# A two-layer hybrid encoder step: value products of two cycles joined, maxima further ahead, output weights split early through memory

## The chip, the cores and the metric

The kernel runs on one core of a Trainium2 chip. The metric is the device time of one execution in microseconds (us), as the median of several runs. A core has a matrix engine (TensorE, PE, with a weight load of its own, PEld), a vector engine (VectorE, DVE), an activation engine (ScalarE, ACT), a general engine (GpSimd, POOL) and an engine that here only issues DMA (SyncE, SP). Each works through its own queue in order and waits on semaphores.

## What is computed

One inference step of one layer for 2048 prompt positions and 8 samples of 16 positions, model width 1024. The layer normalises its input, makes one combined projection, runs three mixers beside each other, and projects their gated outputs back:

```
h = rms_norm(x, norm_g)
fq, fk, fv, fg, ff, su, sg, mq, mg = split_columns(h @ w_in)
fox_out = fox_attend(fq, fk, fv, logf).reshape(B, T, FOX_WIDTH) * jax.nn.silu(fg)
ssm_out = ssm_y * jax.nn.silu(sg)
mem_out = memory_attention(mq, mem_k, mem_v).reshape(B, T, MEM_WIDTH) * jax.nn.silu(mg)
mix = jnp.concatenate([fox_out, ssm_out, mem_out], axis=-1) @ w_out
return x + mix
...
s = einsum(q, k) * HEAD_DIM ** -0.5 + cq - ck          # fox: 8 heads of 64, causal
p = softmax(where(mask, s, -inf));  out = einsum(p, v)
```

The memory attention has four heads of 64 into 256 tokens without a mask. Products of f32 quality are made of three products of rounded halves (high by high, high by low, low by high), so the operands, `w_out` among them, are split into a high half (fp32r) and a low half.

## The kernel before, in words

Three stages follow one another. The projection (up to about 790 us of the profile) goes through passes of 17 position tiles, "visits"; `projection_order` writes down an order of steps that every engine follows, and `beside` hangs other steps on a visit's three parts. The attention of the prompt (790 to 1237 us) and the output product (to the end) are both in `attention_and_output`, whose order comes from `attention_order`.

**The attention's order.** A head has six units (`UNITS`): for the forgetting attention four query groups of four tiles with 4, 8, 12 and 16 key tiles, for the memory attention two groups with two blocks of keys each. That is 44 blocks a head, 352 in all; a cycle is four of them, so a head has 11 cycles and the kernel 88, numbered from 0. The last unit of a head ("fox 12") has cycles 7 to 10 of it; in the last head these are cycles 84 to 87. In a cycle PE does four scores (`scores`: two products each, transposed, keys by queries, L2487 and L2492, and a mask product L2489 on the diagonal), then four maxima (`top`, L2470: the scores again in the other direction, only for their maximum per query), and the value products of the same four blocks (`values`, L2518: 16 products of 64 output columns, 256 queries wide). DVE reduces the maxima (L2828), the negated maxima are turned by PE (`row`, L2481) and copied by ACT (L2607) into a spare row of the query tensor, and the first score of a unit waits for that. ACT then takes the exponential (L2618). The probabilities are summed into denominators by adds (L2788, L2790) on POOL, and for key blocks 2, 3, 6 and 10 of the long units on DVE; `both` (L2841) joins the two sums on DVE, `den` turns them on PE (L2500) and reduces them on DVE (L2847).

**Banks.** `Ring` gives scores, maxima, rows and denominators six banks of PSUM in turn: an entry takes the bank used longest ago and waits until ACT or DVE has emptied it. The exponentials go into 16 slots, four cycles' worth.

**Numbers that set the order.** `LEAD` is how many maxima are issued in the first cycles (four in each later one), and with the 12 issued at three `HOOKS` in the last visits of the projection it sets how far maxima run ahead of scores. `TOGETHER` is over how many cycles the value products are gathered.

**The output weights.** `w_raw` is loaded once (8 chunks of 128x1024). In heads 1 to 4 POOL makes four sums and differences of them per head (`t_sums`, L2734 to L2739), which SP stores. In the last head ACT copies each chunk in two halves into the high part `w_hi` (`w_split`, L2636), which lies over the query and key tensors of the even heads, and POOL subtracts it for the low part (`w_low`, L2743); likewise for the sums (`t_split`, L2648, `t_low_early`, L2747). The first output products, ("product", 0, 0) and (0, 1) (L2586), wait for all of it. Their left side is the mix, loaded tile by tile, turned on PE (`mix`, L2541) and gated on POOL (`gated`, L2721); `first_sum` (L2895) is DVE's sum of the first of them.

**SP's queue.** For every head from 2 on SP issues 7 loads of queries and keys when the head before the last has its scores done (`load_queries_keys`), 8 loads of values and memory tensors (`load_values`), and 4 stores of outputs (`store`).

## Time and profile before

| What | us |
| --- | --- |
| median of 3 runs (1432.9 to 1437.66) | 1434.78 |
| the profiled execution | 1428.78 |
| its span | 1427.1 |
| busy in the span: PE / PEld | 1383.0 / 1101.7 |
| busy in the span: DVE / ACT / POOL | 926.3 / 635.2 / 559.8 |
| product groups of L927, the projection (three groups) | 331.3, 321.7, 234.6 |
| value products L2518 (1216 on the fox values) | 144.8 |
| mean DMA rate over the span | 193 GB/s |

The profile is of one execution. A timeline row gives start, duration, engine, line, operation, output and inputs and how many instructions were merged, and in brackets how long the engine sat idle before and on what. A matmul's duration runs into that of the next one, as they are pipelined; what one costs in a run is the distance between starts.

### The profile page before, as it was taken

How to read it: one execution, taken by the hardware profiler on the slowest of the kernel's cores; microseconds unless marked ns; L12 is line 12 of the kernel's file. 1: busy time of each engine (PE TensorE's matmuls, PEld its weight loads, DVE VectorE, ACT ScalarE, POOL GpSimd, SP SyncE). 2: the span in 40 equal slices, each digit the busy share in tenths (PEclk: the TensorE clock that was granted, in tenths of full speed). 3: DMA queues.
4: the chain of work that ended last, by engine and by line, in shares of the span. 5: the costliest groups of instructions: out<-in, count | busy, mean ns of one | idle time of the engine just before them, and what ended most of it. 6: DMA issues, size and time to landing. Idle time of an engine off the chain costs nothing.

```text
span 1427.1 us, 25010 instructions
## 1 busy us (share of the span) xinstructions
PE 1383.0 (97%) x8510; PEld 1101.7 (77%) x8510; DVE 926.3 (65%) x1772; ACT 635.2 (45%) x1364; POOL 559.8 (39%) x587
## 2 busy tenths in 40 slices
PE   8999989999999999999999999999999999799998
PEld 8999767788877767777777777777777777578886
DVE  4789755692466787665333766676676666697784
ACT  6766423432443364445332555555554556432221
POOL 1121432200033243212000566676775659544442
PEclk9999999999999999999999999999999999899999
DMA  7885699987369679678996945725726514346552
GB/s 230 304 285 189 221 250 243 321 260 211 91 162 326 206 224 301 220 251 261 333 294 187 247 126 113 156 56 116 156 57 130 125 33 126 98 152 217 181 186 86
DMA packets 207565, 275.82 MB, mean 193 GB/s; under 512 B 49424, under 2 KB 146096, under 8 KB 203952
## 3 DMA queue, kind: packets, MB, share of 16 engines
q1 hardware_dynamic: 206400, 274.22, 65.8%
q8 instruction: 70, 1.15, 0.3%
q14 instruction: 55, 0.45, 0.1%
q10 hardware_dynamic: 1040, 0.00, 0.0%
HBM read 186.93 MB, written 86.00 MB: 191 GB/s over the span
## 4 chain that ended last, share of the span: by engine, by line
PE 59%; DVE 5%; issue 2%; POOL 2%; ACT 2%; DMA 1%; SPq 1%; DVEq 0%; ACTq 0%; POOLq 0%
PE in_g L927 13%; PE attn_pv L2518 11%; PE attn_s L2487 6%; PE attn_s L2586 6%; PE attn_s L2492 5%; PE attn_s L2470 5%; PE attn_pv L2586 4%; PE attn_s L2500 2%; PE in_b L1102 1%; POOL in_hv L1810 1%; PE in_b L1054 1%; PE attn_s L2489 1%; PE attn_s L2473 1%; PE attn_s L2541 1%; PE in_b L1157 1%
## 5 line engine op out<-in xcount | busy, mean ns | idle before, releaser
L927 PE MATMUL in_g<-in_wh,in_xh 128*128 128x512 f32 (+2 forms) x904 | 331.3, 380 | 4.9 <-DVE in_wl L1521 1.9
L927 PE MATMUL in_g<-in_wl,in_xh 128*128 128x512 f32 (+2 forms) x904 | 321.7, 369 | 0.0
L2828 DVE TENSOR_REDUCE attn_tops<-attn_s 128x1 f32<-128x512 f32 (+3 forms) x288 | 159.7, 617 | 126.6 <-PE attn_s L2470 110.3
L927 PE MATMUL in_g<-in_wh,in_xl 128*128 128x512 f32 (+2 forms) x904 | 234.6, 378 | 1.4 <-DVE in_xl L1532 1.3
L2790 POOL TENSOR_TENSOR attn_probs<-attn_probs,attn_probs_turned 128x512 f32<-128x512 f32 (+3 forms) x190 | 202.1, 1064 | 86.1 <-ACT attn_probs_turned L2618 64.1
L2618 ACT ACTIVATE attn_probs_turned<-attn_s 128x512 f32<-128x512 f32 (+1 forms) x352 | 161.4, 545 | 144.9 <-PE attn_s L2492 144.6
L927 PEld LDWEIGHTS in_g<-in_wh,in_xh 128*128 128x128 f32 x904 | 165.5, 189 | 39.7 <-issue 6.2
L927 PEld LDWEIGHTS in_g<-in_wl,in_xh 128*128 128x128 f32 x904 | 165.5, 189 | 28.0
L927 PEld LDWEIGHTS in_g<-in_wh,in_xl 128*128 128x128 f32 x904 | 157.8, 189 | 34.4 <-issue 5.2
L1808 POOL TENSOR_SCALAR in_hs<-in_hs 128x8 f32<-128x8 f32 (+1 forms) x53 | 21.3, 402 | 398.6 <-DVE in_hs L1559 398.6
L2518 PE MATMUL attn_pv<-attn_probs_turned,attn_v 128*64 128x256 f32 (+1 forms) x1216 | 144.8, 368 | 0.1
L1219 ACT ACTIVATE in_xh<-in_xu 128x512 fp32r<-128x512 f32 x174 | 99.7, 623 | 57.7 <-DMA in_xu<-scratch_xt 57.7
L2518 PEld LDWEIGHTS attn_pv<-attn_probs_turned,attn_v 128*64 128x64 f32 x1216 | 85.8, 138 | 42.3 <-issue 11.2
L1532 DVE TENSOR_TENSOR in_xl<-in_xu,in_xh 128x512 fp32r<-128x512 f32 x106 | 68.6, 688 | 37.2 <-ACT in_xh L1219 33.7
L1810 POOL TENSOR_TENSOR in_hv<-in_hs,all_neghalf 128x8 f32<-128x8 f32 (+1 forms) x53 | 83.8, 1581 | 4.4
L2487 PE MATMUL attn_s<-attn_qa,attn_ka 128*128 128x512 f32 (+3 forms) x160 | 62.6, 391 | 6.0 <-DVE attn_den L2847 6.0
L2788 POOL TENSOR_TENSOR attn_probs<-attn_probs_turned 128x512 f32<-128x512 f32 x39 | 51.5, 1329 | 39.4 <-ACT attn_probs_turned L2618 39.4
L1260 ACT ACTIVATE in_x_turned<-in_tr 128x512 fp32r<-128x512 f32 (+1 forms) x53 | 27.5, 519 | 85.2 <-PE in_tr L949 76.0
L2487 PE MATMUL attn_s<-all_x,all_y 128*128 128x512 f32 (+3 forms) x160 | 62.1, 388 | 1.6 <-DVE attn_tops L2828 1.6
L2492 PE MATMUL attn_s<-attn_qb,attn_kb 100*128 100x512 f32 (+3 forms) x160 | 61.7, 386 | 0.0
L2492 PE MATMUL attn_s<-all_x,all_y 100*128 100x512 f32 (+3 forms) x160 | 61.0, 381 | 0.0
L1579 DVE TENSOR_TENSOR in_work<-in_g,in_hr 128x512 f32<-128x512 f32 (+1 forms) x53 | 31.4, 593 | 38.4 <-POOL in_hr L1813 37.5
(379 smaller groups left out, 2716.3 us busy)
## 6 DMA issues: line engine op xcount, KB each, us to landing
in_xu<-scratch_xt SPq DMA_DIRECT2D x87, 512.0 KB, 5.5
in_xl<-scratch_xt SPq DMA_DIRECT2D x34, 512.0 KB, 4.6
in_raw<-in_w_in SPq DMA_DIRECT2D x40, 256.0 KB, 5.3
scratch_xt<-in_xu SPq DMA_DIRECT2D x19, 512.0 KB, 4.6
scratch_xt<-in_xl SPq DMA_DIRECT2D x17, 512.0 KB, 4.5
scratch_k<-in_x_turned SPq DMA_DIRECT2D x17, 512.0 KB, 7.0
scratch_q<-in_x_turned SPq DMA_DIRECT2D x17, 512.0 KB, 5.3
in_x_turned<-in_x_prompt SPq DMA_DIRECT2D x16, 512.0 KB, 4.7
```

The lines of the kernel that those rows point to most:

```text
L927: last = X.matmul(g_ps[b][:, 0:m], x, ws[:, c, w0:w0 + m], start=(c == 0 and h == 0 and ws is wh), stop=(c == KC - 1 and h == 1))
L1219: F(xh[:, item_visit[j] % 2, 4 * h:4 * h + 4, :], xu[:, j % 2, 4 * h:4 * h + 4, :], ACT.Copy)\
L1532: V.tensor_tensor(xl[:, v % 3, 4 * h:4 * h + 4, :], xu[:, j % 2, 4 * h:4 * h + 4, :], fl(xh[:, v % 2, 4 * h:4 * h + 4, :]), ALU.subtract). ...
L1810: G.tensor_tensor(hv[:, 0:m], hs[:, 0:m], K.neghalf[:, 0:m], ALU.pow).then_inc(s_hchain, 1)
L2470: last = X.matmul(bank[:, at:at + n, :], qb[h][0:LANE, q], kb[h][0:LANE, keys], start=True, stop=not masked)
L2487: X.matmul(bank[:, part:, :], y2[h][:, keys], x2[h][:, q], start=True, stop=False)
L2492: X.matmul(bank[:, part:, :], y1[h][0:FULL, keys], x1[h][0:FULL, q], start=False, stop=True)\
L2518: last = X.matmul(v_ps[u.n % 2][lane * HD:(lane + 1) * HD, tiles[0] // 2:EACH // 2, :], vals[:, k, :], pt[:, s % SLOTS, tiles[0]::2, :], s ...
L2586: last = X.matmul(y_ps[at], ms[left][:, c, :], ws, start=(begins and c == 0 and k == 0), stop=(ends and c == HALF - 1 and k == 2))
L2618: F(pt[:, s % SLOTS, at:, :], ring_ps[ring.at["scores", s]][:, at:, :], ACT.Exp).then_inc(s_exp, 1)
L2790: E.tensor_tensor(acc[:, part:, :], acc[:, part:, :], mine, ALU.add).then_inc(added[engine], 1)
L2828: V.tensor_reduce(top_parts[:, joined[u.n] % 2, i, k // 4:k // 4 + 1], bank[:, 0:n, :].rearrange("p n k -> p (n k)"), AX.X, ALU.max).then_ ...
```

## The change

It does five things.

1. `TOGETHER` becomes 2: the value products of an even cycle are made with those of the odd one behind it, except in cycles 86 and 87. Denominators are turned at these points only.
2. `LEAD` becomes six for all of the first six cycles, 36 maxima instead of 32, and the three hooks with the first 12 maxima (and row 0) move from behind parts 1 and 2 of the last visit and its end to behind part 2 of the visit before and parts 0 and 1 of the last.
3. In the last unit DVE no longer makes all adds: POOL and DVE share them as in other long units, and `both` for it stands ahead of the first output product, `first_sum` between the first two, `den` behind them.
4. `w_split` and `w_low` work on 16 halves of 128x512, one after each cycle of `W_AT` (17, 20, ... 62, that is in heads 1 to 5). The high half goes into one staging tile `w_stage`, from where POOL subtracts and SP stores it (`store_w`) to memory; SP loads all of `w_hi` back when head 6's scores are done. ACT waits before each copy for the subtraction and the store of the half before (and for the sums made of the chunk).
5. The first two parts of the `t_split` and `t_low_early` move to cycles 78 and 80.

```diff
@@ before_attention
-    for n in range(HOOKS - 1):
-        beside[NV - 1, n + 1] = [("attention", n)]
-    order = projection_order(items, visits, behind, beside) + [("attention", HOOKS - 1)]
+    for n, at in enumerate(((NV - 2, 2), (NV - 1, 0), (NV - 1, 1))):
+        beside[at] = [("attention", n)]
+    order = projection_order(items, visits, behind, beside)
...
-CYCLE, TOGETHER = 4, 1
+CYCLE, TOGETHER = 4, 2
...
-LEAD = (6, 6, 5, 5, 5, 5)
+LEAD = (6, 6, 6, 6, 6, 6)
+W_CHUNKS = (0, 4, 1, 5, 2, 6, 3, 7)
+W_AT = (17, 20, 23, 26, 29, 32, 35, 38, 41, 44, 47, 50, 53, 56, 59, 62)
@@ Sums
-            late = u.head == FOX_HEADS - 1 and u.blocks > 12
-            mine = [k for k, _ in u.scores if u.kind == "fox" and (late or u.blocks > 8 and k in (2, 3, 6, 10))]
+            mine = [k for k, _ in u.scores if u.blocks > 8 and k in (2, 3, 6, 10)]
@@ attention_order
-        if 1 <= n <= KC:
-            order += [("w_split", n - 1, 0), ("w_split", n - 1, 1), ("w_low", n - 1)]
-        if n in (KC, KC + 1):
-            order += [("t_split", n - KC), ("t_low_early", n - KC)]
+        if c in W_AT:
+            order += [(what, W_AT.index(c)) for what in ("w_split", "w_low", "w_out")]
+        if n in (1, 3):
+            order += [("t_split", n // 2), ("t_low_early", n // 2)]
...
-    order += [("product", 0, 0), ("product", 0, 1)] + [("den", n) for n in ended[cycles - 1]]
-    order += [("first_sum", 0), ("t_split", 2), ("t_split", 3), ("mix", 1)]
+    order += [("both", n) for n in ended[cycles - 1]] + [("product", 0, 0), ("first_sum", 0), ("product", 0, 1)]
+    order += [("den", n) for n in ended[cycles - 1]] + [("t_split", 2), ("t_split", 3), ("mix", 1)]
@@ attention_and_output
-        stage = sums_raw[:, 0:2, :]
+        stage, w_stage = sums_raw[:, 0:2, :], sums_raw[:, 2, :]
...
+        def store_w(sp, n):
+            cols = slice(n % 2 * 512, (n % 2 + 1) * 512)
+            sp.wait_ge(s_wh, n + 1)
+            sp.dma_start(D.w_hi[W_CHUNKS[n // 2]][:, cols], w_stage).then_inc(s_w_out, 16)
@@ sync_program, for each head behind store(sp, head - 2)
+                for x in order:
+                    if x[0] == "w_out" and head - 1 == W_AT[x[1]] // (head_end(0) // CYCLE):
+                        store_w(sp, x[1])
@@ sync_program, behind store(sp, FOX_HEADS - 2)
+            sp.wait_ge(s_score, head_end(FOX_HEADS - 2))
+            sp.wait_ge(s_w_out, 16 * 2 * KC)
+            for c in range(KC):
+                sp.dma_start(fl(w_hi[c]), D.w_hi[c]).then_inc(s_w[c % HALF], 16)
@@ tensor_steps, ("product", 0, 0)
-                        pe.wait_ge(s_wl, KC)
+                        pe.wait_ge(s_wl, 2 * KC)
+                        for c in range(HALF):
+                            pe.wait_ge(s_w[c], 16 * 4)
@@ scalar_steps, w_split
-                    act.wait_ge(s_t, 4 * (s % HALF + 1))
-                    act.wait_ge(s_score, head_end(FOX_HEADS - 2))
-                    cols = slice(rest[0] * 512, (rest[0] + 1) * 512)
-                    F(w_hi[s][:, cols], w_raw[:, s, cols], ACT.Copy).then_inc(s_wh, 1)
+                    c, cols = W_CHUNKS[s // 2], slice(s % 2 * 512, (s % 2 + 1) * 512)
+                    act.wait_ge(s_t, 4 * (c % HALF + 1))
+                    if s:
+                        act.wait_ge(s_wl, s)
+                        act.wait_ge(s_w_out, 16 * s)
+                    F(w_stage.bitcast(F32R), w_raw[:, c, cols], ACT.Copy).then_inc(s_wh, 1)
@@ gpsimd_program, w_low
-                    pool.wait_ge(s_wh, 2 * (c + 1))
-                    G.tensor_tensor(w_lo[:, c, :], w_raw[:, c, :], fl(w_hi[c]), ALU.subtract).then_inc(s_wl, 1)
+                    pool.wait_ge(s_wh, s + 1)
+                    G.tensor_tensor(w_lo[:, c, cols], w_raw[:, c, cols], w_stage, ALU.subtract).then_inc(s_wl, 1)
```

How the queues change at three places. First PE between the cycles 6 and 7 of head 0. L2470 and L2473 (L2485 and L2488 after) are maxima, L2481 (L2496) a row, L2518 value products, L2487 and L2492 (L2502 and L2507) scores. Before:

```order
2806 L2470 MATMUL attn_s<-attn_kb,attn_qb 128x512
2807 L2473 MATMUL attn_s<-attn_causr,attn_identr 128x128
2808 L2481 MATMUL attn_s<-attn_identr,attn_negmax 128x128
2809 L2518 MATMUL attn_pv<-attn_probs_turned,attn_v 64x256 x2
2810 L2518 MATMUL attn_pv<-attn_probs_turned,attn_v 64x128
2811 L2518 MATMUL attn_pv<-attn_probs_turned,attn_v 64x256
2812 L2518 MATMUL attn_pv<-attn_probs_turned,attn_v 64x128 x3
2813 L2487 MATMUL attn_s<-all_x,all_y 128x512
2814 L2492 MATMUL attn_s<-all_x,all_y 128x512
```

After:

```order
2811 L2488 MATMUL attn_s<-attn_causr,attn_identr 128x128
2812 L2496 MATMUL attn_s<-attn_identr,attn_negmax 128x128 x2
2813 L2502 MATMUL attn_s<-all_x,all_y 128x512
2814 L2507 MATMUL attn_s<-all_x,all_y 128x512
2815 L2502 MATMUL attn_s<-all_x,all_y 128x512
2816 L2507 MATMUL attn_s<-all_x,all_y 128x512
2817 L2502 MATMUL attn_s<-all_x,all_y 128x512
2818 L2507 MATMUL attn_s<-all_x,all_y 128x512
2819 L2502 MATMUL attn_s<-all_x,all_y 128x512
2820 L2507 MATMUL attn_s<-all_x,all_y 128x512
```

The value products of cycle 6 have gone from between the two cycles to behind the maxima of cycle 7. Second, ACT in cycles 46 to 48: exponentials (L2618, L2635 after), rows (L2607, L2624), copies of values (L2629, L2646). Before:

```order
670 L2618 ACTIVATE attn_probs_turned<-attn_s 128x128
671 L2607 ACTIVATE attn_qb<-attn_s,all_ident 4x128 x4
672 L2629 ACTIVATE attn_out<-attn_pv 128x256
673 L2618 ACTIVATE attn_probs_turned<-attn_s 128x512 x4
674 L2629 ACTIVATE attn_out<-attn_pv 128x256 x2
675 L2618 ACTIVATE attn_probs_turned<-attn_s 128x512 x9
```

After:

```order
658 L2635 ACTIVATE attn_probs_turned<-attn_s 128x128
659 L2635 ACTIVATE attn_probs_turned<-attn_s 128x512 x4
660 L2646 ACTIVATE attn_out<-attn_pv 128x256 x3
661 L2655 ACTIVATE attn_sums_raw<-attn_w_raw 128x512
662 L2635 ACTIVATE attn_probs_turned<-attn_s 128x512 x8
663 L2624 ACTIVATE all_x<-attn_s,all_ident 4x128 x4
```

The copies of three units' values are now together behind the exponentials of cycle 47, and behind them the split L2655 into the staging tile stands ahead of the eight exponentials of cycles 48 and 49. Third, DVE in the last unit: adds (L2788 and L2790; L2807 and L2809 after), joining of the two sums (L2841; L2860), denominators (L2847, L2851; L2866, L2870), low halves of the mix (L2885; L2904), `first_sum` (L2914 after). Before:

```order
1074 L2790 TENSOR_TENSOR attn_acc_v<-attn_acc_v,attn_probs_turned 128x256
1075 L2841 TENSOR_TENSOR attn_acc_v<-attn_acc_v,attn_probs 128x512
1076 L2788 TENSOR_TENSOR attn_acc_v<-attn_probs_turned 128x512
1077 L2790 TENSOR_TENSOR attn_acc_v<-attn_acc_v,attn_probs_turned 128x512 x6
1078 L2847 TENSOR_REDUCE attn_den<-attn_s 128x4
1079 L2851 RECIPROCAL attn_rfox<-attn_den 128x4
1080 L2790 TENSOR_TENSOR attn_acc_v<-attn_acc_v,attn_probs_turned 128x512 x4
1081 L2885 TENSOR_TENSOR attn_qb<-attn_s,attn_qa 128x512
1082 L2885 TENSOR_TENSOR attn_qb<-attn_raw_ka,attn_qa 128x512
1083 L2790 TENSOR_TENSOR attn_acc_v<-attn_acc_v,attn_probs_turned 128x512
1084 L2790 TENSOR_TENSOR attn_acc_v<-attn_acc_v,attn_probs_turned 128x384
1085 L2790 TENSOR_TENSOR attn_acc_v<-attn_acc_v,attn_probs_turned 128x256
```

After:

```order
1072 L2807 TENSOR_TENSOR attn_acc_v<-attn_probs_turned 128x512
1073 L2809 TENSOR_TENSOR attn_acc_v<-attn_acc_v,attn_probs_turned 128x512
1074 L2866 TENSOR_REDUCE attn_den<-attn_s 128x4
1075 L2870 RECIPROCAL attn_rfox<-attn_den 128x4
1076 L2809 TENSOR_TENSOR attn_acc_v<-attn_acc_v,attn_probs_turned 128x512
1077 L2904 TENSOR_TENSOR attn_qb<-attn_s,attn_qa 128x512
1078 L2904 TENSOR_TENSOR attn_qb<-attn_raw_ka,attn_qa 128x512
1079 L2860 TENSOR_TENSOR attn_acc_v<-attn_acc_v,attn_probs 128x512
1080 L2914 TENSOR_TENSOR attn_x_even<-attn_s,attn_x_even 128x512 x2
1081 L2866 TENSOR_REDUCE attn_den<-attn_s 128x4
1082 L2870 RECIPROCAL attn_rfox<-attn_den 128x4
1083 L2880 TENSOR_TENSOR attn_a_raw<-attn_s,attn_probs 128x512
```

Of 16 adds on DVE four are left; the joining sum of this unit is new, and the first sum stands ahead of the last denominators.

## Rows read from the trace of the kernel before

**Rows 1.** Windows: length, busy PE, PEld, DVE, ACT, POOL, PEclk, DMA, GB/s.

```profile
1000.00:1100.00 100.00, 100.00 (x672) 76.43 (x670) 67.14 (x124) 51.40 (x132) 69.63 (x63) 1.00 0.55 118
...
1180.00:1220.00 40.00, 38.01 (x245) 27.16 (x244) 25.05 (x42) 27.93 (x62) 37.58 (x28) 1.00 0.41 114
```

**Rows 2.** Timeline, PE, one cycle: start, us, engine, line.

```profile
896.44 0.22 PE L2481 MATMUL attn_s<-attn_identr,attn_negmax 128*128 128x128 f32 x1
896.60 1.95 PE L2518 MATMUL attn_pv<-attn_probs_turned,attn_v 128*64 128x256 f32 x16
898.47 0.50 PE L2487 MATMUL attn_s<-attn_qa,attn_ka 128*128 128x512 f32 x1
898.81 0.22 PE L2489 MATMUL attn_s<-attn_identr,attn_causr 128*128 128x128 f32 x1
```

**Rows 3.** Waits of the weight loads, 795 to 1211 us: us, times, longest.

```profile
PEld attn_s L2487 <- issue: 23.2, 73, 0.4
```

**Rows 4.** Timeline, PE, end of attention, idle in brackets.

```profile
1219.94 0.84 PE L2500 MATMUL attn_s<-all_ident,attn_acc_v 128*128 128x128 f32 x4 [1.93 <-DVE attn_acc_v L2841]
1220.71 3.37 PE L2518 MATMUL attn_pv<-attn_probs_turned,attn_v 128*64 128x256 f32 x16
...
1234.80 0.69 PE L2487 MATMUL attn_s<-attn_qa,attn_ka 128*128 128x384 f32 x1 [6.00 <-DVE attn_den L2847]
...
1236.99 1.50 PE L2541 MATMUL attn_s<-all_ident,attn_out 128*128 128x128 f32 x6
...
1240.97 0.50 PE L2586 MATMUL attn_s<-all_x,attn_qa 128*128 128x512 f32 x1
...
1249.53 0.47 PE L2586 MATMUL attn_s<-all_x,attn_qa 128*128 128x512 f32 x1 [1.62 <-DVE attn_x_even L2895]
```

**Rows 5.** Timeline, PE and ACT, start of attention.

```profile
791.37 0.50 PE L2487 MATMUL attn_s<-all_x,all_y 128*128 128x512 f32 x1 [1.64 <-DVE attn_tops L2828]
...
787.28 0.69 ACT L1242 ACTIVATE in_work<-in_g,in_half 128x512 f32<-128x512 f32 x1 [6.00 <-PE in_g L927]
789.85 1.12 ACT L2607 ACTIVATE all_x<-attn_s,all_ident 4x128 fp32r<-4x128 f32 x4 [1.88 <-PE attn_s L2481]
```

**Rows 6.** Timeline, DVE, last unit's adds.

```profile
1222.66 11.48 DVE L2790 TENSOR_TENSOR attn_acc_v<-attn_acc_v,attn_probs_turned 128x512 f32<-128x512 f32 x6
...
1234.88 3.06 DVE L2790 TENSOR_TENSOR attn_acc_v<-attn_acc_v,attn_probs_turned 128x512 f32<-128x512 f32 x4
```

**Rows 7.** Timeline, POOL, gating of the third mix tile.

```profile
1249.18 1.04 POOL L2721 TENSOR_TENSOR attn_out<-attn_out,attn_rfox 128x512 f32<-128x512 f32 x1 [16.38 <-DMA attn_out<-scratch_mem_gate]
```

**Rows 8.** Windows, the granted clock: PEclk, the third number from the end.

```profile
1220.00:1224.00 4.00, 4.00 (x20) 2.10 (x20) 3.90 (x2) 0.68 (x1) 4.00 (x2) 0.57 0.01 4
...
1234.80:1238.40 3.60, 3.60 (x15) 3.29 (x15) 2.83 (x5) 1.15 (x3) 0.00 (x0) 0.50 0.02 6
```

**Rows 9.** Timeline, POOL and PE, cycles 16 to 18.

```profile
874.20 4.11 POOL L2790 TENSOR_TENSOR attn_probs<-attn_probs,attn_probs_turned 128x512 f32<-128x512 f32 x3 [3.55 <-ACT attn_probs_turned L2618]
880.14 3.21 POOL L2790 TENSOR_TENSOR attn_probs<-attn_probs,attn_probs_turned 128x512 f32<-128x512 f32 x3 [1.82 <-ACT attn_probs_turned L2618]
...
887.28 1.82 POOL L2739 TENSOR_TENSOR attn_sums_raw<-attn_w_raw,attn_t_raw 128x512 f32<-128x512 f32 x1
...
883.13 0.50 PE L2487 MATMUL attn_s<-attn_qa,attn_ka 128*128 128x512 f32 x1
```

**Rows 10.** Timeline, SP and PE, heads 3 and 4.

```profile
1010.21 0.48 SPq L2229 DMA_DIRECT2D attn_qb<-scratch_q  x1
...
1034.29 0.69 SPq L2262 DMA_DIRECT2D scratch_mem_t<-attn_out  x1
...
1032.10 0.50 PE L2487 MATMUL attn_s<-all_x,all_y 128*128 128x512 f32 x1
```

**Rows 11.** DMA issues, 790 to 1200 us: KB each, us to landing.

```profile
scratch_t<-attn_sums_raw SPq DMA_DIRECT2D x8, 256.0 KB, 2.2
...
scratch_fox_t<-attn_out SPq DMA_DIRECT2D x14, 256.0 KB, 3.7
```

5 lines of the change are left out of this document (3 added, 2 removed).

## The prediction

> **What bounds the kernel now.** I read the page first, then busy time by stretches, the order of time on TensorE, the waits, and the order of time on the other engines. The profiled execution took 1428.8 us for a span of 1427.1 us, 6.0 us under the median of the runs shown, 1434.8 us; the steps below are worked out on the profiled execution, and the difference is taken off the median. In the middle of the attention TensorE (PE) is busy without a break: 100.00 us of 100 [rows 1]. There only less work on PE, or a new wait on it, changes the time; an edit on ACT, DVE, POOL or SP counts only if PE is made to wait or stops waiting. Towards the end of the attention this is over: 38.01 of 40 us, with POOL busy 37.58 [rows 1], and behind it come the long idle stretches of [rows 4]. They are the second place where time can be won.
>
> **1. Cycles joined, 88 value groups become 45.** The value products (a 128x64 tile) stand between products with full 128-column tiles. In the cycle of [rows 2] PE goes from a 128-column product at 896.44 to the first value product at 896.60, 0.16 us, where 128 columns take 0.06 (the 16 value products of 256 columns each start within 1.87 us, 0.117 apiece): 0.10 lost on the way in. Behind the values the first score product holds PE for 0.34 us (898.47 to 898.81), where its 512 columns take 0.23 at that rate: 0.11 lost on the way out. The waits show it too: between 795 and 1211 us the weight load of that product starts late 73 times, 23.2 us in all [rows 3]. 43 groups go, one of them in the last unit, which I work out apart: 42 x 0.20 = 8.4 us. The lower bound is 42 x 0.10, if a new loss from maxima to scores takes half of it back (the trace of before has that seam only once, under a wait); the upper is 8.8. I take 8.4, since each seam is seen in the trace at its size. The adds, exponentials and maxima are unchanged in number, so nothing else is removed here.
>
> **2. First maxima sooner and four more of them ahead.** Before the first scores PE sits idle 1.64 us, until DVE empties a bank [rows 5]. With the maxima ahead of the last product, DVE is through in time; but then the first scores need row 0, which ACT copies only behind its step on the last product. That step starts at 787.28, takes 0.6 us until the next can start, and the four copies take 1.12 us [rows 5]: 2.0 us behind the end of the product at 787.1. The maxima and the row that PE did in between, 2.4 us, are now ahead of the product. So the product ends 2.6 us later and the scores follow 2.0 us behind it with one bank product in the shadow: the wait changes its name, and the time is the same within 0.3 us. The four maxima further ahead cost no work; they give slack to rows in the middle and put six maxima per cycle on DVE in cycles 2 to 5, six banks in back-to-back scores and maxima; I count 0.7 us of waits for it.
>
> **3. The last unit.** Before, the last unit's 16 adds are all DVE's. They wait for DVE to take over POOL's sum of the unit before, which is late because POOL makes eight low halves of the weights among its adds (busy 37.58 of 40 us, [rows 1]); then six adds of full width take 11.48 us, 1.91 each, where four more take 3.06, 0.77 each, once POOL is done [rows 6]. PE waits 1.93, 6.00 and 1.62 us [rows 4]. Behind the first two the granted clock is 0.57 and 0.50 of full speed, the lower of the two levels (1.2 GHz against 2.4) [rows 8]: the values at 1220.71 take 3.37 us for 1.95 [rows 2, 4], 1.42 lost, and the stretch from 1234.80 to 1240.97, 6.17 us [rows 4] at about half clock, loses 3.05. That is 14.0 us. In the changed kernel POOL has no weight halves in the last head, takes 11 adds of the last unit and DVE four. Three adds with a neighbour on DVE take 3.2 us when one is narrow and 4.1 when all are wide [rows 9], against 3.9 us of PE for a cycle without maxima (eight products of 0.23 and the values' 1.95): POOL ends some 3 us behind the last scores, DVE's joining sum at about 4.5, and PE comes to the last transposes only behind two products, 8.1 us behind them. So the cover is over 3 us wide. The first sum moves ahead of the denominators, so the 1.62 goes as well. What is late next: the transposes of the third mix tile need POOL's product, which starts at 1249.18 when a DMA lands [rows 7], 12.2 us behind the end of the last scores at 1237.0 [rows 4]; the loads ahead of it, two of 1 MB among them, still start only with the last scores. PE would get there at 12.1 us and POOL's two products end at 13.8: 1.7 us come back. Net 14.0 - 1.7 = **12.3 us**, between 10 and 14.
>
> The Trainium skill, "SBUF — State Buffer", section "Who interferes with whom", says that a DVE instruction with two SBUF inputs contends with a GpSimd instruction that reads SBUF. Its summary of the shared pair is an exclusive lock for a whole instruction. [Rows 6] agree in kind. By the lock each DVE add beside POOL's would hold POOL up for its whole 0.77 us, where the 4.1 us for three POOL adds hold a part of that already. POOL would fall back by at most 0.8 us in each of three cycles, 2.4 us of a cover of over 3 us, and rival B below would weigh a little more; the sum would stay.
>
> **4. Weight halves in heads 1 to 5, through one staging tile.** 16 ACT copies and POOL subtractions of 128x512 replace 16 copies and 8 subtractions of 128x1024. Their own time is hidden: ACT is busy 51.40 and POOL 69.63 of 100 us [rows 1]. Their waits are another matter, for each stands in ACT's queue ahead of the next cycle's exponentials, and PE can only do four scores and two maxima (2.6 us) before it needs a bank that those exponentials empty. An exponential ends 1.2 us behind the release, so ACT may be 1.4 us late at the start of a cycle at no cost.
> - Cycle 17: the copy waits for four sums on POOL that end at 889.1 [rows 9]. Joined, POOL goes from cycle 16's adds to 17's without its 1.82 us idle: 887.3. Cycle 18 starts at 883.13 [rows 9] less 0.2, or 882.9. So ACT is held until 4.4 us into cycle 18, the copy ends at 5.0, the first exponential at 5.5, where PE wants the bank at 2.6: PE waits 2.9 us.
> - Cycle 47: the copy waits until the half before it is in memory. Its store stands in SP's queue behind the loads of a head, which SP takes 24.8 us to issue (1010.21 to 1034.98) [rows 10], its queue being full. They start when head 3's last scores are done. Cycle 48 starts 21.9 us later (1032.10) [rows 10]; joined, those scores lie 2.0 us further ahead and 0.4 is saved: 23.5. ACT is there at 24.3, SP at 24.8, and the store lands 2.2 us later at the least [rows 11], or 3.7 if it takes as long as a store into a full queue: at 27.0 or 28.5. The exponential ends 1.3 us behind that, PE wants the bank at 26.1: it waits 2.2 to 3.7, I take 2.9.
> - Cycles 26, 38 and 59 meet the same queue, but ACT comes later or SP sooner there: 0.5 us together. Where two rows are copied (twice the 1.12 us of [rows 5]) inside a joined pair, at cycles 20, 42 and 64, 1.0 us.
> - With the 0.7 us of part 2: 2.9 + 2.9 + 0.5 + 1.0 + 0.7 = 8.0 us. Bounds: 0, if ACT's lateness is absorbed, and 16, if each estimate is half of what comes.
> - A wait of 2.9 us may lower the clock behind it. After 1.93 us idle it fell, after 1.64 it did not [rows 5, 8]; a fall cost 1.42 us and 0.24 more on the transposes. I count one of two: 1.7 us, bounds 0 and 3.4.
> - The 4 MB read back start with head 7, when no other head is loaded; before, 4 MB landed while attention ran on. They are needed over 40 us later: nothing. The mix loads behind them come some 10 us later, still ahead of POOL's step in cycle 81.
>
> **Sum.** 8.4 + 12.3 - 8.0 - 1.7 = 11.0 us off: a span of about 1416 us, and **1423.8 us** as a median.
>
> **Rivals.**
> - *A: the waits of part 4 don't reach PE.* For it: PE shows no wait at all between 795 and 1211 us ([rows 3] has late weight loads only); against it: with values held back PE has less to do ahead of the bank. 1423.8 - 9.7 = 1414.1 us.
> - *B: POOL remains late in the last head.* Its work there is some 30 us of the 32 us ahead of the last unit, and PE's transposes for unit 46 need POOL's adds of cycle 83. If gating the first mix tile waits for its loads behind the 4 MB, everything behind it slides; beyond 3 us the last sum is late as well, and the 6.00 us wait with its clock loss comes back: 9.3 us less, 1433.1 us, no change.
> - *C: slower. Each joined pair waits for a bank.* Scores, maxima, scores, maxima follow one another through six banks, while DVE needs 2.4 us for four maxima and up to 1.9 us for an add beside POOL. I find 0.2 to 0.9 us of slack at the third maximum of the second cycle. If that is 0.5 us short in each of 43 pairs, 21.5 us are added: 1445.3 us. It decides from 0.26 us per pair on; above 0.36 the kernel is slower by over 0.3%. Against it: DVE is busy 67.14 of 100 us [rows 1], and the banks that the maxima take were given to the same engine three microseconds before.
> - *D: halfway,* the waits of part 4 twice as long, the store's landing above all: 1431.8 us.
>
> **Chances.** Forecast 0.50, A 0.18, B 0.12, C 0.07, D 0.13. The range goes from a little below A, 1412.5, to just short of D, 1431.0. A measurement of this kernel can tell about 0.3%, 4.3 us, from no change: faster is below 1430.5. The forecast with its own spread (1417 to 1430) and A are there, with a part of D: 0.76. Within 0.3%: B, most of D, the rim of the forecast: 0.17. Slower: C: 0.07.
>
> **What would show it.** Right: a mean of about 4.89 us per cycle for 4.99; "issue" waits of the score weight load about 37 times for 73; PE waits named after ACT's exponential just behind the cycles 17 and 47; POOL's eight 128x1024 subtractions gone from the last head, and no idle PE from the last unit's scores to its first product over 1 us; a wait for row 0 of about 1.6 us at the start. Wrong: many short waits on PE inside the pairs (C); POOL busy without a break before the last unit and its sum late (B); or ACT waiting for SP and PE none the less busy (A).

## The result, and the profile after

| | before | after |
| --- | --- | --- |
| median, us | 1434.78 (1432.9 to 1437.66, 7 runs) | 1448.04 (1442.29 to 1453.31, 7 runs) |
| ratio | | 1.0089, 95% interval 1.0075 to 1.0103 |
| profiled execution, its span | 1428.78, 1427.1 | 1453.31, 1451.3 |
| mean granted clock of that execution | 0.996 | 0.984 |

The kernel became slower by 13.3 us; the forecast was that it would be 11.0 us faster. The two profiles differ by 24 us, more than the medians, because that of before (1428.78 us) lies below all seven executions in the table and that of after is the slowest of its seven. The sizes below are those of the profiled pair.

The page first, the busy lines and the 40 slices of the granted clock:

```profile
PE 1396.3 (96%) x8510; PEld 1120.9 (77%) x8510; DVE 913.5 (63%) x1761; ACT 637.7 (44%) x1364; POOL 572.9 (39%) x606
...
PEclk9999999999999999999999999999989899999999
```

PE does the same 8510 matmuls, but is busy 13 us longer (1383.0 before), though its value products stand in 43 groups fewer: busy time grows where the clock is low. The projection is the same (busy 759.41 us of the first 785, 758.02 before), and from the first output product to the end PE takes 187.7 us for 186.1. All the rest is in the attention, from the first scores behind row 0 to the first product: 791.13 to 1263.59 us here, 791.37 to 1240.97 before [rows 4, 5], 472.5 us for 449.6.

The waits of PE there (us in total, times, longest; the 1.63 us for row 0, the longest at L2507, lie just ahead of the stretch and are not counted in its sum):

```profile
PE attn_s L2485 <- ACT attn_probs_turned L2635: 15.1, 10, 3.6
PE attn_s L2507 <- ACT all_x L2624: 3.0, 3, 1.6
PE attn_s L2515 <- DVE attn_acc_v L2860: 0.9, 2, 0.7
PE attn_s L2496 <- ACT attn_probs_turned L2635: 0.5, 3, 0.2
PE attn_s L2502 <- ACT attn_probs_turned L2635: 0.3, 2, 0.2
```

Before, PE had no wait between 795 and 1211 us. Now maxima wait for a bank that ACT's exponentials have to empty. Six of the ten waits stand behind a split of the output weights and make up 13.9 us: 2.62, 0.83, 2.14, 2.95, 3.56 and 1.82, behind cycles 17, 20, 26, 38, 47 and 59. The largest, on PE, ACT and SP (start, us, engine, line; idle before it in brackets):

```profile
1058.96 1.28 PE L2485 MATMUL attn_s<-all_y,all_x 66*128 66x512 f32 x2 [3.56 <-ACT attn_probs_turned L2635]
...
1057.79 0.63 ACT L2655 ACTIVATE attn_sums_raw<-attn_w_raw 128x512 fp32r<-128x512 f32 x1 [4.52 <-DMA scratch_w_hi<-attn_sums_raw]
1058.33 2.04 ACT L2635 ACTIVATE attn_probs_turned<-attn_s 128x512 f32<-128x512 f32 x4
...
1029.20 0.48 SPq L2232 DMA_DIRECT2D attn_qb<-scratch_q  x1
...
1034.54 13.04 SPq L2247 DMA_DIRECT2D attn_mqa<-scratch_mq  x2
...
1053.81 4.99 SPq L2323 DMA_DIRECT2D scratch_w_hi<-attn_sums_raw  x2
```

Read it from the last row up. SP issues a head's loads from 1029.20 on and is stopped for 13.04 us among them; the store of the staged half is issued at 1053.81, 24.6 us after the first load (24.8 was the forecast). ACT has wanted to overwrite the staging tile since 1053.27 and stands until the store has landed, 3.9 us behind its issue. The four exponentials of the next cycle are queued behind the copy, so PE gets its bank at 1058.96. All of ACT's waits at this line, by what they were for:

```profile
ACT attn_sums_raw L2655 <- DMA scratch_w_hi<-attn_sums_raw: 15.3, 4, 4.5
...
ACT attn_sums_raw L2655 <- POOL attn_sums_raw L2758: 6.1, 2, 3.6
```

Then the clock. Windows of 4 us of PE (length, busy, PEclk, DMA share, GB/s), around the waits of cycles 17 and 47:

```profile
888.00:892.00 4.00, 2.31 (x11) 1.00 0.00 0
892.00:896.00 4.00, 3.07 (x8) 0.50 0.17 66
896.00:900.00 4.00, 4.00 (x22) 0.65 0.00 0
...
1056.00:1060.00 4.00, 1.04 (x2) 0.90 0.32 120
1060.00:1064.00 4.00, 4.00 (x13) 0.50 0.00 1
1064.00:1068.00 4.00, 4.00 (x19) 0.50 0.02 4
1068.00:1072.00 4.00, 4.00 (x31) 0.82 0.00 0
```

At both the clock goes from 2.4 to 1.2 GHz, for 6.8 and for 10.2 us (each window's length times its missing share, over one half). It does so at the waits of cycles 17, 26, 38, 47 and 59, which are all five of more than 1.8 us, and once more at the start, behind the 1.63 us. At cycles 17, 26 and 38 it goes down already in the last 0.6 to 1.6 us of the wait, at the other two 0.3 and 1.4 us behind it. Together PE is at the lower level for 47.8 us of the attention, for 10.2 before. Half of what PE is busy of it is lost: 21.9 us (3.9 of the 47.8 are idle), for 4.7 before.

So the attention of the profiled pair comes out as: waits 18.2 us for 7.9, + 10.3; clock + 17.3; the joining - 6.3 (experiment e20). That is 21.3 of the 22.9 us by which the stretches differ; a rest of about the remaining 1.6 us shows again in e20, and its cause is open. The last unit, the other half of the forecast, did what was expected of it: no wait of PE over 0.25 us from the last unit's scores to the first product.

### The profile page after: what moved, and what is told of

It reads as the page before. It is cut to its first block, busy times and chain, and to the rows that moved or that the text cites. A ratio compares the mean times of both kernels' runs of the same rounds, so it can differ in the third digit from the quotient of the medians.

```text
span 1451.3 us, 25044 instructions
## 1 busy us (share of the span) xinstructions
PE 1396.3 (96%) x8510; PEld 1120.9 (77%) x8510; DVE 913.5 (63%) x1761; ACT 637.7 (44%) x1364; POOL 572.9 (39%) x606
## 4 chain that ended last, share of the span: by engine, by line
PE 49%; SPq 6%; DVE 5%; ACT 4%; issue 3%; DMA 3%; POOL 2%; ACTq 0%; DVEq 0%; POOLq 0%
PE in_g L927 13%; PE attn_pv L2533 8%; PE attn_s L2603 5%; PE attn_pv L2603 4%; SPq L2247 3%; PE attn_s L2502 3%; PE attn_s L2507 3%; PE attn_s L2485 3%; ACT attn_probs_turned L2635 2%; PE attn_s L2515 2%; PE in_b L1102 1%; DMA scratch_w_hi<-attn_sums_raw 1%; POOL in_hv L1810 1%; SPq L2265 1%; PE in_b L1054 1%
## 5 line engine op out<-in xcount | busy, mean ns | idle before, releaser
L2809 POOL TENSOR_TENSOR attn_probs<-attn_probs,attn_probs_turned 128x512 f32<-128x512 f32 (+3 forms) x200 | 215.7, 1079 | 91.9 <-ACT attn_probs_turned L2635 68.5
L2847 DVE TENSOR_REDUCE attn_tops<-attn_s 128x1 f32<-128x512 f32 (+3 forms) x288 | 160.3, 617 | 143.9 <-PE attn_s L2485 123.6
L2635 ACT ACTIVATE attn_probs_turned<-attn_s 128x512 f32<-128x512 f32 (+1 forms) x352 | 162.3, 545 | 103.7 <-PE attn_s L2507 102.5
L2533 PE MATMUL attn_pv<-attn_probs_turned,attn_v 128*64 128x256 f32 (+1 forms) x1216 | 138.2, 369 | 0.0
L2533 PEld LDWEIGHTS attn_pv<-attn_probs_turned,attn_v 128*64 128x64 f32 x1216 | 91.0, 140 | 40.2 <-issue 9.4
L2507 PE MATMUL attn_s<-all_x,all_y 100*128 100x512 f32 (+3 forms) x160 | 63.3, 396 | 3.0 <-ACT all_x L2624 3.0
L2807 POOL TENSOR_TENSOR attn_probs<-attn_probs_turned 128x512 f32<-128x512 f32 x40 | 52.4, 1318 | 29.3 <-ACT attn_probs_turned L2635 29.3
L2502 PE MATMUL attn_s<-all_x,all_y 128*128 128x512 f32 (+3 forms) x160 | 63.2, 395 | 0.2 <-ACT attn_probs_turned L2635 0.2
L2502 PE MATMUL attn_s<-attn_qa,attn_ka 128*128 128x512 f32 (+3 forms) x160 | 62.9, 393 | 0.2 <-ACT attn_probs_turned L2635 0.2
L2507 PE MATMUL attn_s<-attn_qb,attn_kb 100*128 100x512 f32 (+3 forms) x160 | 63.0, 394 | 0.0
L2485 PE MATMUL attn_s<-all_y,all_x 66*128 66x512 f32 (+3 forms) x160 | 49.3, 404 | 12.4 <-ACT attn_probs_turned L2635 12.1
```

Of the source, the lines that this page charges most:

```text
L2485: last = X.matmul(bank[:, at:at + n, :], qb[h][0:LANE, q], kb[h][0:LANE, keys], start=True, stop=not masked)
L2502: X.matmul(bank[:, part:, :], y2[h][:, keys], x2[h][:, q], start=True, stop=False)
L2507: X.matmul(bank[:, part:, :], y1[h][0:FULL, keys], x1[h][0:FULL, q], start=False, stop=True)\
L2533: last = X.matmul(v_ps[u.n % 2][lane * HD:(lane + 1) * HD, tiles[0] // 2:EACH // 2, :], vals[:, k, :], pt[:, s % SLOTS, tiles[0]::2, :], s ...
L2635: F(pt[:, s % SLOTS, at:, :], ring_ps[ring.at["scores", s]][:, at:, :], ACT.Exp).then_inc(s_exp, 1)
L2809: E.tensor_tensor(acc[:, part:, :], acc[:, part:, :], mine, ALU.add).then_inc(added[engine], 1)
```

## Experiments

Ratios are to the kernel before, run beside each kernel on the same chip; its median was 1432.0 (e1, e3, e4, e5), 1434.4 (e9, e10, e11, e13) and 1433.3 us (e14 to e20). Kernels that ran on different chips are compared by these ratios. A trace is one execution of a kernel, and its waits and clock need not be those of the next one.

### Is it the splits, or the joining?

e1_join is the kernel before with `TOGETHER` 2:

```diff
-CYCLE, TOGETHER = 4, 1
+CYCLE, TOGETHER = 4, 2
```

> The kernel before, with the cycles joined in pairs and nothing else of the change. Theory Q (the change lost its time to the splits of the output weights in heads 1 to 5, which stop ACT behind a store or a sum, and to the clock that falls behind each such wait; the joining itself works): 1427 to 1430 us, 5 to 8 us under the kernel before, no new waits of PE in the middle of the attention and a granted clock of 1.00 there. Rival J (the joining itself costs: PE waits for banks inside the pairs, or the joined values pull the clock down): 1440 us or more, with short PE waits in every second cycle.

Measured: 1438.8 us, ratio 1.0038 (1.0024 to 1.0052). Neither theory was right. No wait for a bank in the pairs is longer than 0.2 us, but there are five for a row, and the clock falls at the very start:

```profile
791.23 0.80 PE L2487 MATMUL attn_s<-all_x,all_y 128*128 128x512 f32 x1 [1.64 <-DVE attn_tops L2828]
798.67 0.79 PE L2492 MATMUL attn_s<-all_x,all_y 100*128 100x512 f32 x1 [0.67 <-ACT all_x L2607]
...
944.92 0.50 PE L2492 MATMUL attn_s<-all_x,all_y 100*128 100x512 f32 x1 [0.93 <-ACT all_x L2607]
...
792.00:796.00 4.00, 4.00 (x19) 0.50 1.04 254
...
800.00:804.00 4.00, 4.00 (x13) 0.50 1.03 225
```

Up to 791.2 us this kernel issues the same instructions as the kernel before and waits the same 1.64 us [rows 5], yet here the clock is at its lower level for 17 us and there not at all. The execution of before that was profiled had a mean clock of 0.996; its 20 runs beside this kernel had 0.990 to 0.993. So the profile on which the forecast was built lacked low clock that all 20 have. e18_adders below, which is the kernel before up to the last head, has a fall of 10.2 us at this place in its trace, with a mean clock of 0.991. A fall here is therefore the likely reason for the 6 us between the profile of before and the median; no trace of an ordinary execution of that kernel was kept that would show it.

e9_join_lead adds the lead of the change, six maxima in each of the first six cycles.

> The kernel before with cycles in pairs and six maxima in each of the first six cycles (e1_join with the lead of the change). e1_join showed PE waiting 0.93 us for a row in every second head and 0.67 at the start, 5.3 us in all. Theory L (these waits are a lead that is four banks too short): they go, 1432 to 1435 us, where e1_join had 1438.8. Rival (the row waits come from the pairs as such): 1437 to 1440 us, as e1_join. For the joining by itself both say that a head of 11 cycles takes 54.1 to 54.3 us where it is undisturbed, for 54.88 before: 0.12 us per pair, not 0.20.

Measured: 1434.75 us, ratio 1.0000 (0.9984 to 1.0016). In e1_join the waits for rows were 0.67 and four times 0.93, 4.4 us in all (not the 5.3 of the text above). Two of 0.68 are left, and 0.70 and 0.27 of other kinds: four more maxima of lead are needed as soon as cycles are joined. Joined and with its lead, the kernel is as fast as before, not faster.

e3_spaced is the changed kernel with the splits at other cycles:

```diff
-W_AT = (17, 20, 23, 26, 29, 32, 35, 38, 41, 44, 47, 50, 53, 56, 59, 62)
+W_AT = (18, 20, 23, 29, 31, 35, 40, 42, 46, 51, 53, 57, 62, 64, 68, 73)
```

> The changed kernel with the sixteen splits at cycles 18, 20, 23, 29, 31, 35, 40, 42, 46, 51, 53, 57, 62, 64, 68 and 73: none is ahead of the store of the one before it when that store stands behind the loads of a head in SP's queue, and the first isn't in the cycle of POOL's sums. Work and bytes are the same. Theory Q: the PE waits behind the splits (13.9 us in six places) and five falls of the clock (some 20 us) go: 1413 to 1422 us. Rival J: 1440 us or more. Rival W (the sixteen splits cost by their work on ACT and POOL, wherever they stand): between, 1430 to 1440 us.

Measured: 1420.43 us, ratio 0.9919 (0.9898 to 0.9941), as theory Q has it. The same work and the same bytes, at other places, are worth some 24 us (the difference of the two ratios). Rival J and rival W, the work of the splits wherever they stand, are both out. ACT waits for no store any more, and the first product starts at 1232.43 us, for 1263.59. What is left behind splits are three waits of 0.83 us, where a split and two rows fall into the first cycle of a pair, two of them with the clock low behind them.

e5_c17 moves only the first split, from cycle 17 to 18.

> The changed kernel with only the first split moved from cycle 17 to cycle 18; ACT waited 3.56 us there for POOL's sums and PE 2.62 us, and the clock was at its lower level for about 6.8 us behind it. Theory Q: that wait and that fall go, 5 to 6.5 us: 1441.5 to 1443 us, and the granted clock is 1.00 between 885 and 905 us. Rival J: no change, 1446 to 1450 us, since the fall comes from something else.

Measured: 1438.97 us, ratio 1.0059 (1.0039 to 1.0078), 4.3 us less than the change by the ratios (5 to 6.5 expected, and the two intervals overlap a little); the wait of 2.62 us and its fall are gone from the trace. It doesn't price that wait alone: behind cycle 38 PE waits 0.57 us here and not 2.95, behind cycle 59 1.05 and not 1.82, while the fall at the start lasts 13.7 us for 6.8, and the ten executions range from 1434.5 to 1446.0 us. So the waits at the other splits move when one split moves.

e16_one_wait puts one wait back: e11's places (below), the fourth split at 26 instead of 29. It has the hooks of the change and not those of e11; PE's wait for row 0 is 1.63 us with either.

> e11's places of the splits, with the fourth split at cycle 26 instead of 29, where its wait for a store behind the head loads is back, and the hooks of the change. One such wait by itself. Theory Q: ACT waits some 3.6 us for the store, PE some 2.1, and the clock is at its lower level for 7 us behind it: 5 to 6 us more than e11_odd_sooner, 1423 to 1426 us. Rival J: the wait costs its 2.1 us alone, and the falls in the changed kernel come from joined cycles: 1420 to 1421.5 us.

Measured: 1428.94 us, ratio 0.9974 (0.9957 to 0.9991), for 0.9878 of e11 and 0.9895 of e20, which is the same kernel as e11: 11 to 14 us, and not 5 to 6. The rows show why:

```profile
943.42 0.63 ACT L2655 ACTIVATE attn_sums_raw<-attn_w_raw 128x512 fp32r<-128x512 f32 x1 [9.51 <-DMA scratch_w_hi<-attn_sums_raw]
...
944.59 0.69 PE L2485 MATMUL attn_s<-attn_kb,attn_qb 66*128 66x384 f32 x1 [8.04 <-ACT attn_probs_turned L2635]
...
940.00:944.00 4.00, 0.00 (x0) 0.58 0.54 157
944.00:948.00 4.00, 3.41 (x14) 0.50 0.17 66
```

The split at cycle 21 sits so late in its head that SP, which stores that half ahead of the next head's loads, begins these loads at 914.78 (910.65 in the changed kernel), and all behind them comes later; the store that the split at 26 waits for is issued at 939.29, not 935.57. The wait of 2.14 us became 8.04. With that and the fall behind it (10.2 us at the lower level, 3.9 of them idle, so 3.2 lost), 11 us are told by this trace, what the comparison with e20 gives. Rival J, the wait without a fall, is out: the fall is there, and e4_single (below) has such falls in single cycles too.

### The queue, or the places?

e17_sp_order leaves the splits of the change where they are, and issues a head's first store ahead of the next head's loads and the second among them (`soon` holds the splits in the first six cycles of a head; its definition is left out here, as is the loop over the stores that follow):

```diff
+                for n in soon[:1]:
+                    store_w(sp, n)
                 load_queries_keys(sp, head)
+                for n in soon[1:]:
+                    store_w(sp, n)
                 load_values(sp, head)
```

> The changed kernel with all its splits where they are, but SP's queue in another order: the store of a head's first split ahead of the next head's query and key loads, the second's between those and the value loads. Theory Q: the waits at cycles 26, 38, 47 and 59 (10.5 us of PE) and four falls of the clock go, the wait at cycle 17 for POOL's sums stays: 1422 to 1430 us, and ACT waits for no store for more than 1 us. Rival P (the splits wait because of where they stand among the adds and exponentials, not because of SP's queue): 1440 us or more. If the loads now come too late for the next head, PE waits for DMA at the start of heads 3 to 6: 1435 us or more.

Measured: 1448.86 us, ratio 1.0111 (1.0091 to 1.0131). No faster, yet the question is answered by the rows:

```profile
ACT attn_sums_raw L2661 <- POOL attn_sums_raw L2764: 6.0, 2, 3.6
...
PE attn_s L2491 <- DMA all_y<-scratch_k: 8.0, 2, 6.7
PE attn_s L2491 <- ACT attn_probs_turned L2641: 4.6, 6, 2.6
PE attn_s L2491 <- DMA attn_ka<-scratch_k: 4.0, 1, 4.0
```

ACT waits for no store, so SP's queue was the cause (theory Q, not P). But now the keys come too late, and PE stands 12 us for them at the head's maxima: the third case of what was expected. What this edit saved in ACT's waits it lost in PE's for the keys.

### What the last unit owes to what

e13_spaced_late is e3_spaced with all sixteen adds of the last unit on DVE, as before.

> e3_spaced with the last unit's sixteen adds on DVE alone, as in the kernel before; POOL has no low halves of the weights to make in the last head here either. If DVE's single-handed adds are the cause of the wait for the last sum (1.91 us each beside POOL), PE waits 3 to 6 us behind the last transposes and the clock falls: 1425 to 1431 us. If POOL's halves in the last head were the cause and not who adds, PE waits under 1.5 us: 1420 to 1422 us.

Measured: 1418.92 us, ratio 0.9898 (0.9871 to 0.9925), no slower than e3. DVE's adds (start, us, count):

```profile
1224.33 4.67 DVE L2810 TENSOR_TENSOR attn_acc_v<-attn_acc_v,attn_probs_turned 128x512 f32<-128x512 f32 x6
```

That is 0.78 each where [rows 6] show 1.91 beside POOL. POOL has nothing to do in that stretch, and then it doesn't matter who adds.

e18_adders is the other half: the kernel before with POOL's eleven adds and the new order at the end, the halves still in the last head.

> The kernel before with two edits of the change alone: POOL takes its eleven adds of the last unit, and the end of the order is the changed kernel's. The halves of the weights stay in the last head. Theory H (what frees the last unit is POOL without the halves): POOL is late with its adds as before, 1432 to 1437 us, no change, or slower, and PE still waits 4 us or more in all between the last unit's scores and the first product. Rival A (the division of the adds and the order do it): 1420 to 1426 us.

Measured: 1432.23 us, ratio 0.9989 (0.9975 to 1.0004), no change:

```profile
1213.97 1.65 PE L2469 MATMUL attn_s<-attn_kb,attn_qb 66*128 66x512 f32 x3 [4.29 <-DVE attn_den L2846]
1253.32 1.09 PE L2499 MATMUL attn_s<-all_ident,attn_acc_v 128*128 128x128 f32 x4 [7.29 <-DVE attn_acc_v L2840]
```

The second wait is for the last joined sum, which stands until POOL has done its adds at 1251.6 us, with halves of the weights between them. The first is for a sum of denominators on DVE, which stands behind an add of 128x512 that took 6.81 us (from 1206.50) while POOL went from one instruction to the next without a break. Together they are 11.6 us, where [rows 4] had 9.6 in three waits. Theory H holds: the gain of the last unit comes from the halves that left the last head, and the other two edits give nothing without them.

e10_spaced_single is e3_spaced with single cycles.

> e3_spaced (splits at cycles where no store is awaited) with single cycles. If the joining gives 0.12 us for each of 43 pairs in a kernel without other disturbance, 5 us more than e3_spaced: 1424 to 1428 us. If the joining is worth the 8.4 us of the prediction, 1428 to 1431 us. If it costs as much in waits and clock as it gives, 1418 to 1422 us.

Measured: 1421.2 us, ratio 0.9911 (0.9884 to 0.9938), like e3. It also sizes the last unit without anything joined: from the last head's memory scores to the first product it takes 34.8 us (1200.33 to 1235.13), before 48.75 (1192.22 to 1240.97): 13.95. The forecast's 14.0 hold 1.62 us that lie behind the first product; up to it 12.4 were forecast. And of the 13.95 some 1.0 us is the lead's: this stretch has 8 maxima here and 12 before.

e4_single is the changed kernel with single cycles, all splits where they were.

> The changed kernel with single cycles as before, everything else of the change kept. Theory Q: the waits behind stores stay, the gain of the joining is lost: 1450 to 1456 us, or down to 1440 us if single cycles leave ACT more slack, so that some waits don't reach PE (values lie between the scores then). Rival J: 1425 us or less, with a clock of 0.99 or more.

Measured: 1439.8 us, ratio 1.0053 (1.0038 to 1.0068). It is 5 us faster than the change, not slower: the second case of what was expected. The profiled execution is one of the quick ones of ten (clock 0.995, where they range from 0.987 to 0.995), so it may show fewer falls than most. In it PE's waits behind splits are 4.12, 0.52, 4.94 and 0.81 us (cycles 17, 26, 47 and 59), and none at 38: the number of larger ones goes from five to two, and so does that of the falls. Cycles 26 and 38 are the first of a pair: behind their copies PE has the next scores and no value products to do. So the joining had a part in the loss after all: 5 us by the ratios, and by the trace not through waits of its own but by letting the splits' waits reach PE.

### The start, and the best version

e11_odd_sooner has the splits in second cycles of pairs only (19, 21, 23, 29, 31, 35, 41, 43, 45, 51, 53, 57, 63, 65, 67, 73) and the first maxima one product sooner still; e20_odd_joined is the same kernel again, e19_odd_single the same with single cycles.

> The changed kernel with splits in second cycles of pairs only (19, 21, 23, 29, 31, 35, 41, 43, 45, 51, 53, 57, 63, 65, 67, 73), and the three groups of first maxima one product sooner still. Theory Q: the three waits of 0.83 us that e3_spaced still has behind a split and two rows in one cycle go, with the two short falls of the clock behind them (5.6 us at the lower level), and the 1.63 us for row 0 go to under 0.3: 1412 to 1417 us, for 1420.4 of e3_spaced. Rival: the maxima that are sooner still hold up the last projection product by as much (their banks are emptied by DVE between its own steps): 1418 to 1421 us.

> e11_odd_sooner with single cycles and nothing else. By the head lengths in the traces (54.11 us in e11 where nothing disturbs it, 54.89 in single cycles) the joining is worth 0.14 us per pair, 6.1 us in 43 pairs, less 2.0 us of waits for rows that only joined cycles show. So this kernel should be 3 to 5 us above e20_odd_joined, 1421 to 1424 us. Rival: the clock falls more often or longer at the start in joined cycles and takes the rest: within 2 us of e20.

> The same kernel as e11_odd_sooner, once more, beside e19_odd_single on the same chip: 1416 to 1420 us, ratio 0.986 to 0.990.

Measured: e11 1418.82 us, ratio 0.9878 (0.9845 to 0.9911); e20 1417.4 us, 0.9895 (0.9872 to 0.9918); e19 1418.77 us, 0.9900 (0.9878 to 0.9922). The three waits of 0.83 are gone. Joined against single, on one chip: 1.4 us, within what can be told from nothing, as the rival had it. The traces split this up. Two heads take 108.18 us joined (867.07 to 975.26) and 109.80 single, 0.147 us per pair, 6.3 in 43. But from the first scores to the first product it is 434.4 us for 436.4. Of the 4.3 that are missing, 2.1 are four waits for rows, a sum and a bank that single cycles don't have. The other 2.2 lie mostly in the first fourteen cycles: these take 2.2 us more instead of 1.0 less, and only 1.2 of that are waits. I can't place this rest. The clock is no part of it there: 1.00 in both.

The joining gives less than forecast because it makes a new seam. In e20 the first score product of 512 columns holds PE for 0.34 us behind value products, 0.285 behind a row or the mask of the maxima and 0.23 behind a full maximum (medians between 795 and 1211 us). So about 0.05 us per pair are lost anew, and 0.20 less 0.05 is 0.15, for 0.147 measured.

The wait for row 0 stayed in e11:

```profile
791.14 0.50 PE L2507 MATMUL attn_s<-all_x,all_y 100*128 100x512 f32 x1 [1.63 <-ACT all_x L2624]
...
789.25 0.69 ACT L1242 ACTIVATE in_work<-in_g,in_half 128x512 f32<-128x512 f32 x1 [7.01 <-PE in_g L927]
789.97 1.12 ACT L2624 ACTIVATE all_x<-attn_s,all_ident 4x128 fp32r<-4x128 f32 x4
```

PE has row 0 ready at 785.40 already, and ACT is idle for 7.01 us; but its program has the copies behind its step on the last product. e14_row_sooner moves them ahead of it, and has the hooks of the change again:

```diff
+                if what == "attention":
+                    K.begin[2](act, n[0])
...
+        def scalar_begin(act, n):
+            if n == HOOKS - 1:
...
+                act.wait_ge(*K.end_sample)
+                act.wait_ge(*K.end_split)
+                scalar_steps(act, [("row", 0)])
```

> e11_odd_sooner with the hooks of the change again, and ACT copying row 0 ahead of its step on the last projection product instead of behind it. In e11 PE waited 1.63 us for that row however soon the maxima stood, since ACT's program had the copies behind that step (789.97, the step from 789.25). Theory R: the copies' place in ACT's program is the whole of this wait: it goes, and with it the fall of the clock that follows it in most runs (6.8 us lost in joined cycles, 22 us at the lower level in e11's profile with the one at the end): 1410 to 1416 us, for 1418.8 of e11. Rival: PE then waits for DVE's first maxima as in the kernel before, and the fall stays: 1417 to 1420 us.

Measured: 1417.96 us, ratio 0.9886 (0.9865 to 0.9907), like e11. The row's wait is gone, but a few products later PE stands 1.35 us (to 791.67) for DVE, which still has a step of the projection to do on that bank, and the clock falls behind it in this trace as well. What is waited for has its third name (maxima, row, DVE's last step), at nearly the same time.

e15_row_mix issues the loads of the third mix tile ahead of the two loads of 1 MB.

> e14_row_sooner with the loads of the third mix tile issued ahead of the two loads of 1 MB (the raw T3 and T4), where e3, e10, e11 and the changed kernel have them behind, and PE waits 2.4 to 3.4 us for POOL's product on that tile. If the place in SP's queue is what makes that tile late: that wait falls under 1 us, 2 to 4 us less than e14, with the fall behind it in some runs: 1407 to 1413 us. If it is the time from the free buffer to the landing (7 us and more by itself): within 1 us of e14.

Measured: 1419.65 us, ratio 0.9911 (0.9894 to 0.9927), no gain. POOL's wait for that tile shrinks to 0.65 us, and PE then stands 6.02 us at the product behind it. The loads of 1 MB now come later: ACT has stood 10.96 us for them when it starts to split the first at 1238.45, and DVE's subtraction and sum follow:

```profile
1231.35 1.04 POOL L2745 TENSOR_TENSOR attn_out<-attn_out,attn_rfox 128x512 f32<-128x512 f32 x1 [0.65 <-DMA attn_out<-scratch_mem_gate]
...
1245.98 0.76 PE L2605 MATMUL attn_s<-all_x,attn_qa 128*128 128x512 f32 x1 [6.02 <-DVE attn_probs L2956]
```

The kernel of e11 and e20 is faster than both kernels of the change, by 1.0 to 1.2% against before. Single cycles with the same places (e19) do as well.

## Why the prediction was wrong, point by point

**1. Joining, 8.4 us.** Direction right, size not. Between 795 and 1211 us the late weight loads behind "issue" went from 73 to 36 (37 forecast), but a pair gives 0.147 us and not 0.20: 6.3 us. The step that failed is "I take 8.4": the new seam from maxima to scores takes back a quarter (0.05 us per pair, above); the lower bound had allowed for a half. What the step had no term for is the slack that single cycles gave: rows come too late for the scores, and a copy behind the first cycle of a pair has no value products over it. Net 0 to 2 us where nothing else disturbs (e19, e20), nothing in e9, and 5 us lost in the changed kernel (e4).

**2. First maxima and lead, 0.** Right in kind: the wait changed its name to row 0 and was 1.63 us for 1.6, and the first scores behind it stand 0.24 us sooner. The 0.7 us for the lead were half of what came, and it was of another kind: two waits for rows, 0.68 and 0.67 us. They belong to the joining and not to the lead, for the single cycles of e4, e10 and e19 have the lead and no such wait. What the sum put at nothing is the fall of the clock at this place, which the trace of before didn't have: 3.1 us lost in the changed kernel's trace, and 5 to 8 us in those of e1, e5, e9, e11, e13, e16 and e18.

**3. Last unit, 12.3 us.** Right in mechanism and nearly in size. Up to the first product 12.9 us came for 12.4 forecast (e10: 13.95 less the 1.0 of the lead). The third mix tile is late as said, with a wait of 2.40 us for 1.7 forecast; from the first product to the end 1.6 us were lost where 0.1 net were forecast (1.7 less the 1.62 that went). That makes about 11.3 for 12.3, with part of the two misses cancelling. The text named the true cause, POOL without halves. The share of the adds, on which it spent much of its working, turned out to matter neither way (e13, e18).

**4. Halves in heads 1 to 5, 8.0 + 1.7 us.** Here the forecast was lost. Cycle 17: 2.62 us for 2.9. Cycle 47: 3.56 for 2.9, the store landing 3.9 us behind its issue, above the 2.2 to 3.7 taken from [rows 11]. Double rows: 0.83, 0.17 and 0.17 us for 1.0. But **cycles 26, 38 and 59 "meet the same queue, but ACT comes later or SP sooner there: 0.5 us together"** took 2.14, 2.95 and 1.82, 6.9 us. The reading of the two queues was right, for SP did issue these stores when or before ACT wanted the tile: at 935.57 for 935.56, at 999.65 for 1002.21 and at 1120.37 for 1120.53. What the step left out is the landing, which took 3.5, 5.15 and 4.5 us, so that ACT stood 3.61, 2.69 and 4.43 us. The four are one case, a split behind the store that is behind a head's loads. They should have been priced alike, not one in full and three with a rest.

And **"I count one of two: 1.7 us"** for the clock. It fell five times of five, and stayed low for 6.8 or 10.2 us each time, 2.6 to 5.1 us lost apiece, not 1.7: 18.9 us, with the start 21.9. The 1.7 was taken from the shorter of two falls in [rows 8], though the other cost 3.05 us already. Of all steps this is the largest miss.

**The rivals.** None gave the result. C had the right sign and nearly the size (1445.3), but for another reason: there are hardly any waits inside pairs, as the waits above show. D doubled the waits of part 4, which was about their true size, but kept one fall of the clock. B didn't come: there is no wait of PE for POOL's sums in the last head. The chance of 0.07 for slower came from looking for it in one place only; a rival "every head has one split behind the store that is behind its loads" was to be had from [rows 8, 10]: with cycle 17 five waits of 2.5 us and five falls of 1.42 to 3.05 us are 20 to 28 us, against 20.7 gained by the forecast: no change or slower.

**The base.** The sum was made against an execution with a clock of 0.996. Its 6.0 us to the median were noted and not asked about. A fall of the clock at the start, which that execution lacked, would be of this size (half of its length is lost), though this is argued and not shown. The falls there last 14 to 17 us in e1, e5, e9, e11, e13 and e16, 3 to 10 in e10, e14, e15, e18 and the change, and there is none in the profiled execution of e3, e4, e17, e19 and e20. Whether joined cycles make it longer (the six long ones are all joined) wasn't settled.

## What to carry to other kernels

A helper's instruction that may wait stands in front of everything behind it on its engine: price each such wait by what the queue of the one it waits for has ahead of it (here 25 us of SP issuing loads, then 4 us until the store lands), give all equal cases the same price, and put the instruction where that queue is known to be empty; that was worth 24 us here and cost nothing. Where TensorE has been busy without a break, add to a wait of 2 us the clock behind it: 2.6 to 5.1 us here. And before a profile is taken as the base, compare its granted clock with that of the other runs; here 0.996 against 0.990 to 0.993 went with 6 us of the time.
